# Relative-position bias read shifted from replicated vectors and added by VectorE; dilated-attention heads taken in pairs with turned outputs

## The reference, cut to what matters

```python
# first stack, both layers (20 heads with a bias; scores (q, k) of one head):
s = q @ k.T * scale + table[bucket(q_pos - k_pos)]      # depends on q_pos - k_pos alone
p = softmax(where(k_pos <= q_pos, s, NEG)); y = p @ v

# second stack, layer 0: dilated attention, 16 heads of 64, three groups g = (window, dilation)
for g, (window, dilation) in enumerate(((128, 1), (512, 4), (2048, 16))):
    s_g = q_g @ k_g.T * 64**-0.5 + rel_bias_g[bucket((k_pos - q_pos))]   # inside the group's window
    o_g, lse_g = softmax_and_denominator(s_g, v_g)
o = sum_g softmax(lse)_g * o_g                           # = one softmax over all three groups' keys
out = o.reshape(256, 1024) @ w_out
```

## Time and profile before

| | |
|---|---|
| median of 3 runs | 3060.45 us (3059.64 to 3062.14) |
| the profiled execution's own time | 3062.16 us |
| its span in the trace | 3060.4 us |
| mean granted TensorE clock | 0.976 of full |
| PE busy | 2904.5 us (95%) |
| DVE busy | 1683.4 us (55%) |
| ACT busy | 1222.1 us (40%) |
| POOL busy | 88.2 us (3%) |
| HBM read, written | 485.47 MB, 1.19 MB (159 GB/s over the span) |

### The profile page before, as it was taken

How to read it: one execution, slowest core, us unless ns; L and a number is a source line. 1 busy time by engine, 2 the same in 40 slices (tenths; PEclk the granted TensorE clock), 3 DMA queues, 4 the chain that set the end, 5 groups by cost and what they waited for, 6 DMA issues and landing times.

```text
span 3060.4 us, 46670 instructions
## 1 busy us (share of the span) xinstructions
PE 2904.5 (95%) x19462; PEld 2616.1 (85%) x19462; DVE 1683.4 (55%) x2543; ACT 1222.1 (40%) x1725; POOL 88.2 (3%) x135
## 2 busy tenths in 40 slices
PE   7999799999999979999999999999999998997998
PEld 7988788799899878879989989996998998883798
DVE  5555466455655536636565554444556555552555
ACT  4443344244444434424444443323444443441443
POOL 1000000000000000000010001100000000000000
PEclk9999899999999989999999999999999999998999
DMA  6544233445455424346555544333454544431453
GB/s 234 186 177 160 109 126 143 159 158 184 170 186 185 174 104 145 125 159 222 185 169 184 186 164 136 132 132 116 169 185 163 184 185 152 161 145 62 156 186 125
DMA packets 49047, 488.50 MB, mean 160 GB/s; under 512 B 6480, under 2 KB 6576, under 8 KB 10520
## 3 DMA queue, kind: packets, MB, share of 16 engines
q1 hardware_dynamic: 43192, 470.44, 42.0%
q0 software_dynamic: 5728, 16.25, 1.8%
HBM read 485.47 MB, written 1.19 MB: 159 GB/s over the span
## 4 chain that ended last, share of the span: by engine, by line
PE 86%; DVE 7%; ACT 4%; issue 2%; DMA 1%; POOL 0%; DVEq 0%; ACTq 0%; SPq 0%; POOLq 0%
PE ps L794 64%; PE ps L845 14%; ACT ring_hi L1408 2%; DVE ring_lo L1725 2%; PE ps L810 1%; PE ps L1244 1%; PE ps L1053 1%; PE ps L1262 1%; DMA ring<-stream_dram 1%; PE ps L1252 1%; DMA norm_g<-norm_gT_dram 1%; DVE ring_lo L1791 1%; PE ps L1239 0%; PE ps L1159 0%; ACT ring_hi L1453 0%
## 5 line engine op out<-in xcount | busy, mean ns | idle before, releaser
L794 PE MATMUL ps<-uTh,ring_hi 128*128 128x256 f32 x4176 | 1202.3, 288 | 20.7 <-DVE qkT L1840 7.1
L794 PE MATMUL ps<-uTl,ring_hi 128*128 128x256 f32 x4176 | 1184.7, 284 | 0.0
L794 PE MATMUL ps<-uTh,ring_lo 128*128 128x256 f32 x4176 | 1184.2, 284 | 0.0
L794 PEld LDWEIGHTS ps<-uTh,ring_hi 128*128 128x128 f32 x4176 | 804.4, 193 | 48.2 <-issue 17.8
L794 PEld LDWEIGHTS ps<-uTl,ring_hi 128*128 128x128 f32 x4176 | 804.4, 193 | 7.6 <-issue 0.5
L794 PEld LDWEIGHTS ps<-uTh,ring_lo 128*128 128x128 f32 x4176 | 803.7, 192 | 0.0
L1791 DVE TENSOR_TENSOR ring_lo<-ring,ring_hi 128x2048 fp32r<-128x2048 f32 x174 | 399.0, 2293 | 242.7 <-ACT ring_hi L1453 242.7
L1725 DVE TENSOR_TENSOR ring_lo<-ring,ring_hi 128x3072 fp32r<-128x3072 f32 (+1 forms) x100 | 297.3, 2974 | 325.2 <-ACT ring_hi L1408 325.1
L1446 ACT ACTIVATE work_all<-work_all 128x256 f32<-128x256 f32 x176 | 73.6, 418 | 756.0 <-DVE work_all L1779 756.0
L1408 ACT ACTIVATE ring_hi<-ring 128x3072 fp32r<-128x3072 f32 (+1 forms) x100 | 245.4, 2454 | 300.6 <-DMA ring<-stream_dram 153.9
L1453 ACT ACTIVATE ring_hi<-ring 128x2048 fp32r<-128x2048 f32 x174 | 330.7, 1901 | 1.7 <-DMA ring<-stream_dram 1.5
(11 more groups left out here) (278 smaller groups left out, 2834.0 us busy)
## 6 DMA issues: line engine op xcount, KB each, us to landing
ring<-stream_dram SPq DMA_DIRECT2D x299, 1536.0 KB, 6.4
mlaT_all<-bias_vectors POOLq DMA_DIRECT2D x32, 96.0 KB, 2.9
bias<-gains_dram POOLq DMA_DIRECT2D x5, 512.0 KB, 7.6
yR<-bias_vectors POOLq DMA_DIRECT2D x1, 2048.0 KB, 10.5
mlaT_all<-bias_vectors POOLq DMA_DIRECT2D x32, 64.0 KB, 2.9
row<-ret_const_dram POOLq DMA_DIRECT2D x1, 1280.0 KB, 5.7
h<-x_rows_dram POOLq DMA_DIRECT2D x2, 512.0 KB, 11.8
yR<-gains_dram POOLq DMA_DIRECT2D x2, 512.0 KB, 9.8
```

What stands on the lines that cost most here:

```text
L794: m = pe.matmul(out_, lhsT, rhs, start=start, stop=stop, **kw)
```

## The change

The bias vectors are stored to DRAM replicated: 128 copies of each of the 21 vectors of the first stack (already scaled by 8), 64 copies of each of the 16 of the dilated stage. A read whose partitions step by one element less than a row then gives each partition its vector shifted the other way, which is the order that the scores need. So both flip matrices, the flip matmuls of both places and `copy_bias` go; the first stack's tables are read straight into `bias`.

In the dilated stage a step s is now both heads of a pair and one block of 128 queries: 16 steps. The PE issues `dilated_turn(s - 1)`, `dilated_scores(s)` with the two heads' matmuls in alternation, four pieces of the next pair, `dilated_values(s - 1)`. VectorE adds bias and scores and takes the maximum in one instruction (into `biased_2`), negates the maximum in a second, and after the exponential scales the probabilities by the reciprocal of their sum. ScalarE copies the turned probabilities, which VectorE did before. `dilated_values` has v as the stationary operand (64 columns) and the probabilities as the moving one (128 columns), so its output is already turned: one ScalarE copy for each pair puts it into `mT_2`, the transposes after the last unit go, and `out_project` waits for each pair by itself. The part of the diff below leaves out the lines that it takes from the functions printed above, and the semaphores' names.

```diff
-        mT_2 = row[:, :, :].rearrange("p a b -> p (a b)")[:, 0:KD * SEQ].rearrange("p (k t) -> p k t", k=KD)
         flatY = yR[:, :, :, :].rearrange("p a b c -> p (a b c)")
+        mT_2 = flatY[:, 0:KD * SEQ].rearrange("p (k t) -> p k t", k=KD)
...
-        hankel_2 = flatM[:, 0:2560].rearrange("p (n c) -> p n c", n=4)
-        flip_2 = flatM[:, 2560:2688]
+        bias_2 = flatM[:, 0:2560].rearrange("p (n c) -> p n c", n=4)
+        biased_2 = xn_flat[:, 0:1024].rearrange("p (b c) -> p b c", b=2)
...
-        vecs_2 = nc.dram_tensor("bias_vectors_2", (16, NV_2), F32, kind="Internal").ap()
-        vecs = nc.dram_tensor("bias_vectors", (21, 512), F32, kind="Internal").ap()
+        vecs_2 = nc.dram_tensor("bias_vectors_2", (16, 64, NV_2), F32, kind="Internal").ap()
+        vecs = nc.dram_tensor("bias_vectors", (21, P, 512), F32, kind="Internal").ap()
...
+        def dilated_out(hp):
+            return (mT_2[:, hp, :].rearrange("p (j r) -> p r j", r=4),
+                    ps[:, 4 + hp % 2, 0:SEQ].rearrange("p (r j) -> p r j", r=4))
...
-            def bias_flips(a):
...
+            def dilated_scores(s):
+                hp, qt = s // 2, s % 2
                 b = hp % 2
...
+                if qt == 0:
+                    pe.wait_ge(*piece_copied(PIECES_DIL + 8 * hp + 5))
+                if s:
+                    pe.wait_ge(biased_2_ready, 2 * s)
+                for g in range(N_GROUPS):
+                    for j in range(2):
+                        r = slice(64 * j, 64 * j + 64)
+                        q = qkD[r, b, 2 * g, qt * P:(qt + 1) * P]
+                        k = qkD[r, b, 2 * g + 1, :] if g == 0 else qkD[r, b, 2 * g + 1, qt * P:(qt + 1) * P]
+                        o = ps[:, j, 0:256] if g == 0 else ps[:, j, 128 * (g + 1):128 * (g + 2)]
+                        m = mm(o, q, k, True, True)
+                        if g == N_GROUPS - 1:
+                            m.then_inc(scores_2, 1)
...
+            def dilated_turn(s):
+                for j in range(2):
+                    pe.wait_ge(normed_2, 2 * s + j + 1)
+                    if s:
+                        pe.wait_ge(pT_2_ready, 2 * s)
+                    for n in range(4):
+                        last = pe.transpose(ps[:, 2 + j, n * P:(n + 1) * P], probs[:, j, n * P:(n + 1) * P], ident)
+                    last.then_inc(turned_2, 1)
...
+            def dilated_values(s):
+                hp, qt = s // 2, s % 2
+                b = hp % 2
+                if qt == 0:
                     for g in (PIECES_DIL + 8 * hp + 6, PIECES_DIL + 8 * hp + 7):
...
+                        pe.wait_ge(*piece_copied(g))
+                    if hp >= 2:
+                        pe.wait_ge(stored_2, hp - 1)
+                pe.wait_ge(pT_2_ready, 2 * s + 2)
                 for n, (g, kt) in enumerate(((0, 0), (0, 1), (1, qt), (2, qt))):
...
+                    for j in range(2):
+                        last = pe.matmul(ps[64 * j:64 * j + 64, 4 + hp % 2, qt * P:(qt + 1) * P],
+                                         vD[:, b, kt, g * P + 64 * j:g * P + 64 * j + 64], probsT[:, j, n * P:(n + 1) * P],
+                                         start=n == 0, stop=n == 3, skip_group_check=True)
...
+                for s in range(NS2 + 1):
+                    if s:
+                        dilated_turn(s - 1)
+                    if s < NS2:
+                        dilated_scores(s)
+                    hp = s // 2 + 1
                     if hp < 8:
...
+                        dilated_pieces(c0, hp, range(4 * (s % 2), 4 * (s % 2) + 4), p)
+                    if s:
+                        dilated_values(s - 1)
+                pe.wait_ge(pT_2_ready, 2 * NS2)
+                out_project(c0 + 24, lambda k, tt: mT_2[:, k, tt * P:(tt + 1) * P], KD, (stored_2, 1))
...
+                for s in range(NS2 + 1):
+                    if s:
+                        for j in range(2):
+                            act.wait_ge(turned_2, 2 * s + j - 1)
+                            if s > 1:
+                                act.wait_ge(out_2, s - 1)
+                            act.activation(probsT[:, j, :], ps[:, 2 + j, :], ACT.Copy).then_inc(pT_2_ready, 1)
+                    if s < NS2:
+                        for j in range(2):
+                            x = small[:, 2 * (s % 2) + j, :]
+                            act.wait_ge(max_2_ready, 2 * s + j + 1)
+                            act.activation(probs[:, j, :], biased_2[:, j, :], ACT.Exp, bias=x[:, 2:3],
+                                           accum_out=x[:, 4:5]).then_inc(exp_2_done, 1)
+                    if s > 2 and s % 2:
+                        act.wait_ge(out_2, s - 1)
+                        dst, src = dilated_out((s - 3) // 2)
+                        act.activation(dst, src, ACT.Copy).then_inc(stored_2, 1)
+                    hp = s // 2 + 1
+                    if hp < 8:
+                        for n in range(4 * (s % 2), 4 * (s % 2) + 4):
+                            copy_2(PIECES_DIL + 8 * hp + n, dilated_copy)
+                            done_dilated(8 * hp + n, take_high)
+                act.wait_ge(out_2, NS2)
+                dst, src = dilated_out(7)
+                act.activation(dst, src, ACT.Copy).then_inc(stored_2, 1)
...
+                later = []
+                for s in range(NS2):
+                    hp, qt = s // 2, s % 2
+                    sm = small[:, 2 * (s % 2):2 * (s % 2) + 2, :]
+                    for j in range(2):
+                        head = 2 * hp + j
+                        if qt == 0:
+                            dve.wait_ge(bias_2_in[head % 4], 64 * (head // 4 + 1))
+                        dve.wait_ge(scores_2, 2 * s + j + 1)
+                        if s:
+                            dve.wait_ge(exp_2_done, 2 * s)
+                        first, table = P * (1 - qt), bias_2[:, head % 4, :]
+                        parts = bass.AP(tensor=table.tensor, offset=table.offset + first,
+                                        ap=[table.ap[0], [384 - first, 2], [1, 256]])
+                        dve.tensor_tensor_reduce(biased_2[:, j, :].rearrange("p (a c) -> p a c", a=2),
+                                                 ps[:, j, :].rearrange("p (a c) -> p a c", a=2), parts, 1.0, NEG,
+                                                 ALU.add, ALU.max, accum_out=sm[:, j, 0:1]).then_inc(biased_2_ready, 1)
+                        dve.wait_ge(biased_2_ready, 2 * s + j + 1)
+                        dve.tensor_scalar(sm[:, j, 2:3], sm[:, j, 0:1], -1.0, None, ALU.mult).then_inc(max_2_ready, 1)
+                    for c in later:
+                        take_low(c)
+                    later = []
+                    for j in range(2):
+                        dve.wait_ge(exp_2_done, 2 * s + j + 1)
+                        link(dve.reciprocal(sm[:, j, 8:9], sm[:, j, 4:5]))
+                        dve.tensor_scalar(probs[:, j, :], probs[:, j, :], sm[:, j, 8:9], None, ALU.mult)\
+                            .then_inc(normed_2, 1)
+                    if hp + 1 < 8:
+                        for n in range(4 * qt, 4 * qt + 4):
+                            copy_2(PIECES_DIL + 8 * (hp + 1) + n, dilated_copy)
+                            done_dilated(8 * (hp + 1) + n, later.append if n == 7 else take_low)
+                for c in later:
+                    take_low(c)
...
-            def copy_bias(a):
...
+            parts = [(0, 8, vec_sb[0:8, 0:512]), (8, 13, vec_sb[0:13, 512:1024])]
+            for first, count, x in parts:
+                pool.dma_start(vecs[first:first + count, :, :],
+                               x.unsqueeze(1).to_broadcast([count, P, 512])).then_inc(vec_stored, 16)
+            for n, (first, count, x) in enumerate(parts):
+                pool.wait_ge(vec_stored, 32)
+                pool.dma_start(bias[:, first:first + count, :],
+                               bass.AP(tensor=vecs.tensor, offset=first * P * 512 + P - 1,
+                                       ap=[[511, P], [P * 512, count], [1, SEQ]])).then_inc(bias_in, 16)
...
-                    pool.wait_ge(scores_2, 2 * (head - 3))
+                    pool.wait_ge(biased_2_ready, 4 * ((head - 4) // 2) + 4)
                 for a in range(2):
-                    dst = hankel_2[64 * a:64 * a + 64, head % 4, :]
-                    o = head * NV_2 + a * P + 1
+                    dst = bias_2[64 * a:64 * a + 64, head % 4, :]
+                    o = head * 64 * NV_2 + (1 - a) * P + 64
...
+                pool.dma_start(vecs_2[:, :, o:o + w], vec_2_sb[32 * n:32 * n + 16, 0:w].unsqueeze(1)
+                               .to_broadcast([16, 64, w])).then_inc(vec_2_stored, 16)
...
```

More of the change, by code:

```diff
@@ L269, in build @@
         gated = [work_all[:, 2304:2560], work_all[:, 2048:2304]]
-        flip = flatM[:, 1280:1280 + P]
         lamb = flatM[:, 1408:1920].rearrange("p (l n d) -> p l n d", l=DEPTH, n=4)
@@ L363, in build @@
         vec_2_stored = sem("vec_2_stored")
```

(36 more changed lines are left out.)

160 lines of the change are left out of this document (17 added, 143 removed).

## The result

The changed kernel takes 3074.99 us (median of 6 runs, 3072.15 to 3077.05), the kernel before 3060.34 in 6 runs beside it. The ratio is 1.0046, 95% interval 1.0034 to 1.0057: slower by 14.7 us, where 54.6 us less had been forecast. The profiled execution took 3077.05 us, its span is 3075.2, the mean granted clock 0.966.

What follows compares the result with a forecast made beforehand. The PE bounds the kernel, with 86% of the span. The dilated stage gives 46.5 us and the first stack's flips 8.1, together 54.6, so 3060.45 becomes 3006 us; range 2988 to 3030.

Steps and rivals of the forecast that it cites:

- The replicated vectors: Larger stores of bias vectors, 5.5 MB and 6.3 MB, each in an FFN, would cost nothing.
- The criterion, landing less what a slot can bear: FFN weight loads, issued 17 us before use with a split of at most 6.1, may take 10.9 us to land.
- the stores slow the weights: Rival: stores lift weight landings to 16, some eight slots lose 3 us each, at most 25; 3015 to 3031, chance 0.05.
- PE's own work in the dilated stage: A two-head step takes 3.13 us beside its four pieces, where two units cost 6.72; heads overlap.
- without overlap 28: Rival: the two heads' matmuls in the dilated stage do not overlap, +28 us, 3034; chance 0.05.
- New waits: Dilated steps: PE waits for VectorE's piece copies, 1.3 us in six even steps, 3.9 in step 0, none in odd; 11.7.
- Step 0: First dilated step: a take_low ahead of the bias delays the first piece's copy, so PE waits 3.9 us.
- The end of the stage: Dilated steps 14 to 16 have no pieces to cover the latency and take 12.9 us.
- The first stack's flips: Removing the first stack's flip matmuls and VectorE's two copies into bias gives 8.1 us, bounds 6 and 8.7.
- The clock falls: Rival: the clock falls; behind earlier waits 56 matmuls ran at full speed, chance 0.08.
- Slower than before: Rival: VectorE and ScalarE bound every dilated step with pieces, adding at least 3.9 us each; 3069 for 4.5, chance 0.03.

Runs made afterwards that it cites:

- e12_spread16: Changed kernel with the second stack's stores reading every eighth partition of another tile, 64 copies each: 3058.68 us, ratio 0.9991.
- e13_close16: Changed kernel with the second stack's stores reading the first 16 partitions of that same other tile, 64 copies each: 3077.26 us, ratio 1.0051.
- e9_cut_not_waited: Changed kernel with the replicated stores cut in pieces of 16 copies, none of them waited for: 3072.44 us, ratio 1.0037.
- e2_paced: Changed kernel with the replicated stores cut in pieces of 16 copies, each waited for before the next: 3016.93 us, ratio 0.9851.
- e6_heads_in_turn: Changed kernel with the two heads' matmuls of scores and values issued one head after the other, not in alternation: 3084.97 us, ratio 1.0075.
- e5_one_copy: Changed kernel with each bias vector stored once and tables read stepping forward, the reversal left out: 3016.21 us, ratio 0.9855.
- e11_waited_64: Changed kernel with the replicated stores cut in pieces of 64 copies, each waited for: 3043.0 us, ratio 0.9942.

## Why the prediction was wrong

**The replicated vectors: the step that failed.** The step is a cost put at nothing: the stores of the replicated vectors took 0 in the sum and cost 62.3 us in the two FFNs. Of the 69 us between the forecast of 3006 and 3075 they are all but 7; the dilated stage has 5.5 of the rest and the flips 1.6. "I take nothing for them" stood on the earlier trace rows: full engines at 413 GB/s and a load that still landed in 7.7. From them followed about 200 GB/s to spare, and queues that share. Both readings were wrong for this transfer. The rate of full engines is not one number: the stores filled them at about 100 GB/s (window 30 to 40), because their source lay on 8 to 16 neighbouring partitions (shown for the second stack by e12_spread16 against e13_close16; for the first stack no run moved the source, and only the rates agree). And the loads did not get their share at once but waited behind what was queued (e9_cut_not_waited against e2_paced). The earlier trace rows was a near row by size only; gain rows are read from DRAM, the vectors from 8, 13 and 16 partitions, and the kernel before had of such sources only 0.1 MB. The form of the source, which the diff shows (`vec_sb[0:8]`, `vec_2_sb[32 * n:32 * n + 16]`), was there to see; what it costs, only the runs showed. By an estimate from the 100 GB/s found, 11.8 MB are 118 us of full engines.

The criterion, landing less what a slot can bear, had the right form and one term too large. I took 6.1 for the split from the earlier trace rows, which are rows of the projections; in an FFN it takes 1.92 + 2.30 = 4.2 (L1414 and L1764 in the chain through FFN 0), so a load may take 12.8 and not 10.9. Landing less 12.8 gives 29.2 and 7.4 for FFN 0, and 9.7 and 5.3 for FFN 4: 51.6 (with 10.9 it would be 59.2). The stands were 62.3 less the clock's 9.6 (1.6, 2.8, 2.4 and 2.7 at the four rows of 48 matmuls behind them), 52.7. My rival "the stores slow the weights" had the mechanism with landings of 16 and at most 25 us, and a chance of 0.05; it was sized too small, as loads landed in 42.0, 20.2, 22.5 and 18.1, and on the wrong side of the outcome.

How many engines a store kept busy is not the main cause. In e2_paced one store of 8 vectors ran alone from 27.2 to 31.4 and from 34.4 to 38.4 us, and the DMA share was 0.51 and 0.50 of 16 engines, at 54 and 53 GB/s. In e9_cut_not_waited two such pieces landed at a time (36.5 and 37.6, 47.0 and 47.7 us) and kept 95% of the engines busy, again at 54 GB/s. Nearly twice the busy share gave no more rate; that the 8 partitions set it is my estimate from that and from the second stack's runs. The store of 13 vectors, alone beside the weights in the changed kernel, had 43.9% (73 to 81 us) and 23.3% (100 to 114 us) of the engines (queue q0), and no view here splits the engines. The second stack's stores, of 16 vectors, kept 97% of the engines busy at 101 GB/s in the window 1620 to 1630.

**PE's own work in the dilated stage: right.** A pair without waits is 32.24 us against a forecast of 25.81 + 2 x 3.13 = 32.07. The heads overlap; heads in turn cost 10.0 (e6_heads_in_turn), so "without overlap 28" was nearly three times too much.

**New waits: right in place, a little small.** Even steps 1.74 instead of 1.3. Odd steps none, as forecast. `take_high` starts at 1900.29, 0.7 behind the start of the scores, since the release comes with the end of their first matmul; I had placed it at their start. Step 0 was forecast at 3.9; the run that removes its cause gained 5.2 (3005.51 to 3000.27). Of that the fallen clock has 1.7 (7.47 for 48 matmuls instead of 5.81); the stand itself is 3.56 in the changed kernel's trace.

**The end of the stage: right**, 13.2 (2102.43 to 2115.63) against 12.9. The stage gave 41.0 instead of 46.5: 6 x 0.44 from the even steps, 7 x 0.17 from the PE, 1.7 of clock and 0.3 at the end are 5.8, less 0.3 for the smaller stand of step 0.

**The first stack's flips: right**, 8.2 for 8.1, less 1.5 of clock, 6.5.

**The clock falls** was a rival of 0.08. It came true in step 0 (1.7, at a granted clock of 0.77 from 1873.8 to 1881.3 us, against 0.56 behind the idle time of the earlier trace rows) and in the first stack (1.5, at 0.64), and four times in the FFNs, behind the stands (0.79, 0.66, 0.70 and 0.67). At the end of the dilated stage it stayed away in the changed kernel's trace and came in others (see below).

**Slower than before** was a rival of 0.03 at 3069, close to the 3075 measured. That is luck of the number: it wanted 3.9 more in every step with pieces from VectorE and ScalarE, and the waits are 1.74 in even steps and none in odd ones.

**What a version without the store trouble gives** is the test of the rest: 3060.45 - 41.0 - 6.5 = 3013 was to be expected from the marks, e2_paced and e5_one_copy measured 3016.9 and 3016.2. In e2_paced most of the difference is the clock at the end of the dilated stage: the last values take 1.97 instead of the changed kernel's 1.09, and the 56 matmuls of `out_project` behind them 25.93 instead of 24.23, 2.6 together; the granted clock was 0.50 from 2052 to 2054 us and 0.60 from 2054 to 2058, where the changed kernel has 1.00 (2115.6 to 2119). In e5_one_copy the two take 1.97 and 26.23. It isn't all that moves: that trace is of the fastest of its four runs (3013.0), and its first stack is 2.9 shorter than the changed kernel's, 1.5 of it because the 25 matmuls behind the lambdas take 3.24 again. Why the clock falls there in some versions and not in the changed kernel's trace stays open.

## What to carry to other kernels

Price a DMA by where its partitions stand (the runs here show it for the source): 16 neighbouring ones as source filled all 16 engines at about 100 GB/s, 16 spread ones gave 196, and a row of the same bytes on 128 partitions says nothing of them. A background transfer that nobody waits for can still stop the program through the engines that it shares: keep little of it queued at once (here pieces of 0.25 to 0.5 MB, each waited for by the engine that has time), and compare the landing of the loads that matter with what their users can bear. When a stage with unchanged code gets slower, marks along the chain of waits find it at once, before any theory.

## What the runs showed of the hardware

- The DMA engines are shown busy (95 to 101%) at 54, 100, 196 and 359 GB/s, for stores alone from the first 8, the first 16, every eighth of, and all 128 partitions. From the first 8 the rate was 54 GB/s with 51% of the engines busy (e2_paced, 27.2 to 31.4 us) and with 95% (e9_cut_not_waited, 40 to 60 us): the busy share did not tell the rate.
- A weight load on another queue landed about when the store piece queued ahead of it did: after 6.3 to 8.0 us behind pieces of about 8 us (e2_paced), after up to 20.9 behind pieces of about 24 (e11_waited_64). With 5.5 MB of stores queued ahead it took 42.0, and one of the two stores was still under way then. Cutting the backlog without waiting left 32.4.
- Two heads of 64 partitions issued one after the other took 1.5 times as long as in alternation (values 1.51 us instead of 1.02), not twice.
- Behind a stand of 7.6 us the next 48 matmuls took 8.59 us instead of 5.75, behind one of 29.5 us 7.39. The longer stand did not cost more clock. The mean granted clock of 60 to 80 us was 0.67.
